# A two-layer hybrid decoder: norms by token halves, the last two FFN tiles projected down together

## The chip, the cores and the metric

The kernel runs on one core of a Trainium2 chip. The metric is the device time of one execution in microseconds. Before the change it is 2683.03 us, the median of 3 runs (2682.59 to 2683.53). The engines are PE (TensorE, matmuls), DVE (VectorE), ACT (ScalarE), POOL (GpSimd) and SP (SyncE, which here only issues transfers). Each has its own instruction queue, works it off in order, and waits for the others at semaphores.

## What is computed

Two layers over 1024 tokens with 1024 features, float32:

```python
for layer in range(DEPTH):                                   # DEPTH = 2
    hn = rms_norm(h, norm_mix_g[layer])
    h = h + hybrid_mixer(hn, ...)                            # @ w_in (3072 columns), attention and conv, @ w_out
    hn = rms_norm(h, norm_ffn_g[layer])
    h = h + conv_glu_ffn(hn, w_up[layer], conv_ffn_w[layer], w_down[layer])
return rms_norm(h, final_g)

def rms_norm(x, g, eps=1e-6):
    return x * rsqrt(mean(x * x, axis=-1) + eps) * g
def conv_glu_ffn(h, w_up, conv_w, w_down):                   # D_FF = 2816, 22 tiles of 128
    g, u = split(h @ w_up, 2)
    return (silu(causal_dwconv(g, conv_w)) * u) @ w_down
```

So there are five norms: before each mixer, before each FFN, and one over the result.

## The kernel before

**Layout.** `h` holds the state with features on the 128 partitions: `h[:, m, :]` is feature tile m (of 8), with all 1024 tokens along it. A matmul takes a 128 x 128 weight block and 512 tokens, so each token half t has its own PSUM bank (there are 8 banks of 512 float32). Every float32 product is made of three passes: w_hi x_hi, w_hi x_lo, w_lo x_hi (`three_pass`, L425 to L427). POOL splits each weight tile, 128 x 1024, into w_hi and w_lo (`split`, L349 and L351); there are two slots, so a tile is split only when the tile two places before it has been used up, and SP loads the raw tile into `stage` once its slot is free (L284). ACT makes x_hi = round(h * g) (`head_tile`, L665) and DVE makes x_lo = h * g - x_hi (`absorb`, L870).

**A norm.** The factor rstd per token is applied after the projection, as DVE takes a bank out (`evacuate`, L856: bank * rstd_all). So projection can begin before rstd is known, but its result can't leave PSUM. The order of a norm (`start_normed` on PE, `start_norm` on DVE): ACT squares the 8 feature tiles into 8 scratch tiles (L668), POOL adds them in five steps (`start_sums`, `end_sums`, L358), DVE does the last two adds (L900, L902), PE sums over the partitions by 8 one-column matmuls (`sum_squares`, L466), DVE computes rsqrt by 12 tiny operations (`rsqrt`, L881 to L894) and spreads it along a diagonal (L906), PE multiplies that by ones (`spread`, L473), and ACT copies the outcome to `rstd_all` (L672). Meanwhile PE does, for the first two weight tiles, all w_hi x_hi and w_lo x_hi (64 matmuls, L488 and L490), then waits for the sum, does w_hi x_lo (32, L499), and the spread. A third and a fourth tile follow (`project`), and need the slots of the first two.

**Start of a layer.** DVE takes out q and k of unit 0, rotates both (`rotate`, L914 to L919), takes out v, splits q and k (`keep_k`, `keep_rests`, up to L937) and raises `cur_ready`, for which the first scores wait. Then attention follows, where PE mixes scores, transposes and projections in a fixed order. At the very start ACT issues the loads of x by 8 feature tiles (L822), does two sines and an exponential for rotary tables and lambda, and then squares and heads in turn.

**FFN.** For tile f, PE projects gate and up (2 x 48 matmuls), DVE takes out the gate, ACT applies the centre tap (L809) and DVE the other two (L1103), ACT the silu (L814), DVE multiplies by up (L1114), ACT rounds to `mix_hi` (L816), DVE makes `mix_lo` (L1118, `mix_ready`). PE then projects down (`down`): 8 feature tiles x 2 halves x 3 passes, and DVE adds each to `h` (`add_down`, L875). Down of tile f - 1 is issued behind the projections of tile f, and DVE's 8 adds stand ahead of the product of tile f. Down of the last tile, 21, has nothing in front of it. Its banks are `DOWN` (2 to 7, in pairs).

**The end.** After the last down come squares, sums, rsqrt, spread, rstd, 8 output operations (L1199) and 8 transfers (L331).

## Time and profile before

| | |
|---|---|
| median of 3 runs | 2683.03 us |
| the profiled execution: its time / its span | 2682.59 / 2680.8 us |
| PE busy | 2531.5 us, 94% |
| DVE, POOL, ACT busy | 60%, 30%, 23% |
| granted PE clock, mean | 0.978 |
| chain that ended last | PE 82%, DVE 12%, ACT 3%, issue 2% |

PE's busy time counts matmuls from issue to their modelled end; those in a row overlap, so the distance between two starts is the figure to read. The granted clock is a share of 2.4 GHz: 0.50 is 1.2 GHz. In the 40 slices of the page (67 us each), PE stands at 6 tenths in the first and 4 in the last, and at 8 or 9 elsewhere. The time outside the span is 1.8 us.

### The profile page before, as it was taken

To read this page: it belongs to the slowest core of one execution; us is meant where nothing else is said; L and a number is where in the kernel's file an instruction comes from. 1 tells how busy PE (TensorE), PEld (TensorE's weight loads), DVE (VectorE), ACT (ScalarE), POOL (GpSimd) and SP (SyncE) were. 2 spreads that over 40 slices of the span, in tenths; PEclk is the share of its full clock that TensorE was granted. 3 is DMA by queue.
4 is the path that set the end of the run, shared out by engine and by line. 5 is a ranking of instruction groups with operands and counts; after the bars stand their busy time and mean duration, and the time that the engine had idled before them with its cause. 6 is when DMAs were issued, how large, how long until landed. Compare 5 with 4: busy or idle time off the path is not lost.

```text
span 2680.8 us, 29574 instructions
## 1 busy us (share of the span) xinstructions
PE 2531.5 (94%) x12006; PEld 2105.2 (79%) x12006; DVE 1603.8 (60%) x1979; ACT 624.3 (23%) x1161; POOL 815.4 (30%) x437
## 2 busy tenths in 40 slices
PE   6999998899999999999889999979999999999994
PEld 4888887777888888888678888868788888888883
DVE  6545677535556665566674467763465555666555
ACT  3344444321010010000224334443210001001002
POOL 4221213142333333333432111222433333333332
PEclk9999999999999999999999999989999999999997
DMA  3000001211111111111210000121111111111111
GB/s 129 32 24 32 24 32 40 74 48 40 47 48 48 50 53 47 47 48 47 102 40 24 32 24 32 32 79 41 38 45 54 48 48 48 48 50 52 48 40 63
DMA packets 50583, 127.32 MB, mean 47 GB/s; under 512 B 4496, under 2 KB 22032, under 8 KB 50448
## 3 DMA queue, kind: packets, MB, share of 16 engines
q1 hardware_dynamic: 47856, 120.05, 13.6%
q10 hardware_dynamic: 2592, 5.38, 0.5%
q8 instruction: 96, 1.57, 0.2%
q14 instruction: 39, 0.32, 0.0%
HBM read 116.76 MB, written 8.39 MB: 47 GB/s over the span
## 4 chain that ended last, share of the span: by engine, by line
PE 82%; DVE 12%; ACT 3%; issue 2%; POOL 0%; DMA 0%; DVEq 0%; ACTq 0%; POOLq 0%
PE ps L425 24%; PE ps L427 24%; PE ps L426 24%; PE ps L539 3%; DVE x_lo L870 3%; PE ps L526 2%; DVE h L916 2%; PE ps L499 1%; PE ps L513 1%; ACT prob L750 1%; PE ps L514 1%; DVE h L914 1%; DVE prob L950 1%; PE ps L466 1%; DVE q_next L917 0%
## 5 line engine op out<-in xcount | busy, mean ns | idle before, releaser
L425 PE MATMUL ps<-x_hi,w_hi 128*128 128x512 f32 x2304 | 910.8, 395 | 17.3 <-POOLq L354 8.9
L427 PE MATMUL ps<-x_hi,w_lo 128*128 128x512 f32 x2304 | 901.0, 391 | 0.0
L426 PE MATMUL ps<-x_lo,w_hi 128*128 128x512 f32 x2304 | 900.4, 391 | 0.0
L349 POOL CAST w_hi<-stage 128x1024 fp32r<-128x1024 f32 (+1 forms) x198 | 206.5, 1043 | 1749.2 <-PE ps L427 1661.2
L351 POOL TENSOR_TENSOR w_lo<-stage,w_hi 128x1024 fp32r<-128x1024 f32 (+1 forms) x198 | 522.0, 2636 | 15.8
L425 PEld LDWEIGHTS ps<-x_hi,w_hi 128*128 128x128 f32 x2304 | 434.4, 189 | 110.3 <-POOLq L354 13.1
L427 PEld LDWEIGHTS ps<-x_hi,w_lo 128*128 128x128 f32 x2304 | 434.2, 188 | 91.8
L426 PEld LDWEIGHTS ps<-x_lo,w_hi 128*128 128x128 f32 x2304 | 434.9, 189 | 87.0
L875 DVE TENSOR_TENSOR h<-ps,h 128x1024 f32<-128x1024 f32 x352 | 431.0, 1224 | 78.7 <-PE ps L427 38.8
L425 PE MATMUL ps<-q_split,w_hi 128*128 128x512 f32 x704 | 277.0, 393 | 10.7 <-DVE q_split L1118 10.7
L427 PE MATMUL ps<-q_split,w_lo 128*128 128x512 f32 x704 | 275.8, 392 | 0.0
L426 PE MATMUL ps<-q_split,w_hi 128*128 128x512 f32 x704 | 275.8, 392 | 0.0
L816 ACT ACTIVATE q_split<-k_next 128x1024 fp32r<-128x1024 f32 x44 | 46.7, 1061 | 720.9 <-DVEq L1116 720.9
L856 DVE TENSOR_TENSOR q_next<-ps,rstd_all 128x512 f32<-128x512 f32 x112 | 77.0, 691 | 226.4 <-PE ps L427 202.9
L1103 DVE SCALAR_TENSOR_TENSOR k_next<-padded,vec,k_next 128x1024 f32<-128x1024 f32 x88 | 176.7, 2008 | 57.8 <-ACT k_next L809 56.2
L856 DVE TENSOR_TENSOR padded<-ps,rstd_all 128x512 f32<-128x512 f32 x88 | 60.0, 685 | 200.7 <-PE ps L427 183.2
L750 ACT ACTIVATE prob<-prob,neg_top 128x128 f32<-128x128 f32 (+3 forms) x192 | 147.1, 770 | 125.2 <-DVE neg_top L950 124.9
L539 PE MATMUL ps<-v_cur,padded 128*128 128x64 f32 (+1 forms) x1152 | 152.9, 276 | 14.1 <-ACT padded L709 11.4
L425 PEld LDWEIGHTS ps<-q_split,w_hi 128*128 128x128 f32 x704 | 133.3, 189 | 41.5 <-issue 11.5
L539 PEld LDWEIGHTS ps<-v_cur,padded 128*128 128x128 f32 x1152 | 144.1, 193 | 20.5 <-ACT padded L709 14.6
L427 PEld LDWEIGHTS ps<-q_split,w_lo 128*128 128x128 f32 x704 | 133.1, 189 | 27.9
L426 PEld LDWEIGHTS ps<-q_split,w_hi 128*128 128x128 f32 x704 | 133.3, 189 | 27.3
(136 smaller groups left out, 2264.6 us busy)
## 6 DMA issues: line engine op xcount, KB each, us to landing
stage<-stream SPq DMA_DIRECT2D x180, 512.0 KB, 3.2
stage<-stream SPq DMA_DIRECT2D x16, 448.0 KB, 4.6
h<-x_t ACTq DMA_DIRECT2D x8, 512.0 KB, 9.3
h<-x_t SPq DMA_DIRECT2D x8, 512.0 KB, 3.3
saved_h<-h SPq DMA_DIRECT2D x8, 512.0 KB, 2.8
h<-saved_h SPq DMA_DIRECT2D x8, 512.0 KB, 3.3
out_t<-h SPq DMA_DIRECT2D x8, 512.0 KB, 3.0
stage<-stream SPq DMA_DIRECT2D x16, 64.0 KB, 4.7
```

Source lines behind the costliest of these rows:

```text
L349: pool.tensor_copy(w_hi[:, s, wide], stage[:, s, wide]).then_inc(pool_seq, 1)
L351: pool.tensor_tensor(w_lo[:, s, wide], stage[:, s, wide], w_hi[:, s, wide].bitcast(f32), ALU.subtract)\
L425: pe.matmul(out, w_hi[:, s, w], hi, start=start, stop=False)
L426: pe.matmul(out, w_hi[:, s, w], lo, start=False, stop=False)
L427: return pe.matmul(out, w_lo[:, s, w], hi, start=False, stop=stop)
L526: ended = pe.transpose(ps[:, TURNED, b * P:(b + 1) * P], prob[:, g % 2, j, (b0 + b) * P:(b0 + b + 1) * P], eye[:, :])
L539: ended = pe.matmul(ps[:, HEAD, at:at + wide], turned_groups[count % 2][:, (b - b0) * P:(b - b0 + 1) * P], v_cur[:, b, dims], start=b == 0 ...
L750: act.activation(scores, scores, ACT.Exp, bias=neg_top[:, g % 2, j:j + 1], scale=-1.0, accum_out=total[:, g % 2, j:j + 1]).then_inc(exp_do ...
L856: dve.tensor_tensor(out[:, halves_of_t[t]], bank(b), rstd_all[:, halves_of_t[t]], ALU.mult)\
L870: dve.scalar_tensor_tensor(x_lo[:, m, :], h[:, m, :], g_of(m), x_hi[:, m, :].bitcast(f32), ALU.mult, ALU.subtract).then_inc(x_lo_ready, 1)
L875: dve.tensor_tensor(h[:, m, :], bank(DOWN + 2 * (m % pairs), 2), h[:, m, :], ALU.add)\
L1103: dve.scalar_tensor_tensor(k_next[:, :], padded[:, TAPS - 1 - back:TAPS - 1 - back + SEQ], tap, k_next[:, :], ALU.mult, ALU.add).then_inc( ...
```

## The change

- **Norms by token halves.** Heads, rests, squares, sums, rsqrt, spread and rstd are done for tokens 0 to 511 (t = 0) and 512 to 1023 (t = 1) apart. PE's new order in `start_normed`: heads of tiles 0 and 1 for half 0, their rests, heads and rests of tile 0 for half 1, heads of tile 1, sum of half 0, rests of tile 1, and then the third tile's projection into banks 6 and 7 (`THIRD`), with spread of half 0, sum of half 1 and spread of half 1 put between its k steps. A first weight tile is free for its successor when three halves are done. rsqrt of half 1 (`end_norm`) comes on DVE after half 0 of the first tiles has been taken out.
- **Who adds squares.** At a layer's start DVE adds all eight (`partial(..., 1)`, seven half adds, each waiting for the one before). Before the FFN and at the end, POOL adds the first six and DVE two (`SUMMED` = 6); before the FFN POOL does this ahead of the splits of the first two FFN tiles.
- **The last two FFN tiles together.** `last_down`: down of tiles 20 and 21 is accumulated in one bank per feature tile, all 8 banks, first half 0 of tile 20 and of 21, then half 1; DVE adds halves. `mix_hi` and `mix_lo` alternate between two buffers.
- **The start.** x is loaded by SP in eight transfers, each of two feature tiles and one half, the first between the first two weight tiles; ACT does heads and squares before its sines. The rotary angles are computed on DVE between the two halves of `absorb`; lambda is computed after unit 0's q and k are ready. POOL clears the unused halves of k_lo. Between the FFN and layer 1 ACT does heads ahead of squares, by halves (`prepare_next`).
- **The end.** In the last layer, half 1's rows use banks 0, 1, 4, 5 in a ring, each row ended before the next; half 0's sum, spread and outputs lie between them. Outputs read the spread from PSUM, and leave in 16 transfers.

```diff
-            plan.append((layer, "tile", projection_tile(unit, group), "halves", halves + (2 if n == 0 else 0)))
+            plan.append((layer, "tile", projection_tile(unit, group), "halves", halves + (1 if n == 0 else 0)))
...
+            if f == F_TILES - 1:
+                plan.append((layer, "tile", down_tile(f - 1), "layers", layer + 1))
+            elif f:
                 downs += KT
                 plan.append((layer, "tile", down_tile(f - 1), "downs", downs))
-        downs += KT
+        downs += 2 * KT
...
+        ROW_BANKS, RING = (2, 3, 0, 1, 4, 5, 6, 7), (0, 1, 4, 5)
+
+        NORM, THIRD = (SCORE, SCORE + 1), (TURNED, HEAD)
...
-                    sp.wait_ge(add_done, (layer * F_TILES - 1) * KT + m + 1)
+                    sp.wait_ge(add_done, half_added(layer - 1, m, 1))
...
+            def load_x(t, m):
+                rows = x_t[m * P:(m + 2) * P, halves_of_t[t]].rearrange("(k p) t -> p k t", p=P)
+                sp.dma_start(h[:, m:m + 2, halves_of_t[t]], rows).then_inc(x_in[t][m // 2], 16)
+
             n = 0
             for layer in range(DEPTH):
-                for _ in range(2):
-                    load(n)
-                    n += 1
+                load(n)
+                if layer == 0:
+                    load_x(0, 0)
+                load(n + 1)
+                n += 2
                 if layer:
                     save_h(layer)
+                else:
+                    for t in range(2):
+                        for m in range(0, KT, 2):
+                            if t or m:
+                                load_x(t, m)
...
+            def sum_squares(norm, halves, parts):
+
+                for m in range(0, SUMMED, 2):
+                    for t in halves:
+                        pool.wait_ge(squares_ready[t], KT * norm + m + 2)
+                    add_squares(parts, m, m + 1)
+                    if m:
+                        add_squares(parts, 0, m)
                 pool.sem_inc(pairs_ready, 1)
...
+                for n in range(len(PROJECTIONS) + 1):
                     split()
+                    if layer == 0 and n == 1:
+
+                        pool.memset(k_lo[high, 0, :].bitcast(f32), 0.0).then_inc(zeros_ready, 1)
+                        pool.memset(k_lo[low, 1, :].bitcast(f32), 0.0).then_inc(zeros_ready, 1)
+                        pool.wait_ge(zeros_ready, 2)
                 pool.wait_ge(half_done, layer * LAYER_HALVES + PROJECTED)
                 for m in SPLIT_BY_POOL:
                     split_mix(layer, m)
                 for _ in range(len(OUT_TILES) - 1):
                     split()
-                sums_and_splits()
-                for _ in range(3 * F_TILES - 2):
+                sum_squares(2 * layer + 1, range(2), slice(0, SEQ))
+                for _ in range(3 * F_TILES):
                     split()
-            start_sums()
-            end_sums()
+            for t in range(2):
+                sum_squares(2 * DEPTH, (t,), halves_of_t[t])
...
+            def last_down(layer):
+                f = F_TILES - TOGETHER
+                tiles = (next_tile(), next_tile())
+                ready(tiles[0])
+                pe.wait_ge(mix_ready, seen(mix_ready))
+
+                pe.wait_ge(add_done, half_added(layer, 0, 0) - 1)
+                for m, b in enumerate(ROW_BANKS):
+                    take_bank(b)
+                    down_part(f, tiles[0], m, 0, b, True)
+                ready(tiles[1])
+                pe.wait_ge(mix_ready, seen(mix_ready))
+                for m, b in enumerate(ROW_BANKS):
+                    down_part(f + 1, tiles[1], m, 0, b, False).then_inc(down_done, 1)
+                if layer < DEPTH - 1:
+                    for m, b in enumerate(ROW_BANKS):
+                        pe.wait_ge(add_done, half_added(layer, m, 0))
+                        ended = down_part(f, tiles[0], m, 1, b, True)
+                    ended.then_inc(first_of_two, 1)
+                    for m, b in enumerate(ROW_BANKS):
+                        down_part(f + 1, tiles[1], m, 1, b, False).then_inc(down_done, 1)
+                else:
+                    for m in range(KT):
+                        if m == 2:
+                            sum_squares(0)
+                        if m == 5:
+                            spread(0)
+                        b = RING[m % len(RING)]
+                        if m < len(RING):
+                            pe.wait_ge(add_done, half_added(layer, ROW_BANKS.index(b), 0))
+                        else:
+                            pe.wait_ge(add_done, half_added(layer, m - len(RING), 1))
+                        down_part(f, tiles[0], m, 1, b, True)
+                        down_part(f + 1, tiles[1], m, 1, b, False).then_inc(down_done, 1)
+                down_tiles[0] += 2 * KT
...
+                for i in range(2):
+                    heads_of_x(i, 0)
+                for i in range(2):
+                    rests_of_x(i, 0)
+                heads_of_x(0, 1)
+                rests_of_x(0, 1)
+                heads_of_x(1, 1)
+                sum_squares(0)
+                rests_of_x(1, 1)
+                n = next_tile()
+                project_half(n, 0, THIRD[0], {3: lambda: spread(0), 6: lambda: sum_squares(1)})
+                if n < len(PROJECTIONS):
+                    pe.wait_ge(lam_exped, 1)
+                project_half(n, 1, THIRD[1], {5: lambda: spread(1)})
...
+                project()
+                project()
+                last_down(layer)
+            sum_squares(1)
+            spread(1)
...
             def prepare_loaded():
-                for m in range(KT):
-                    act.wait_ge(x_in[m], 16)
-                    square_tile(m, m)
-                    if KT // 2 <= m < KT - 1:
-                        head_tile(m - KT // 2, gain[:, m - KT // 2:m - KT // 2 + 1])
-                for m in range(KT // 2 - 1, KT):
-                    head_tile(m, gain[:, m:m + 1])
+                for t in range(2):
+                    for m in range(KT):
+                        act.wait_ge(x_in[t][m // 2], 16)
+                        head_tile(m, t, gain[:, m:m + 1])
+                    for m in range(KT):
+                        square_tile(m, m, t)
 
             def prepare_ffn(layer):
                 done = layer * LAYER_HALVES + PROJECTED + OUT_EARLY
+                last = OUT_ORDER[-1]
                 for p, m in enumerate(OUT_ORDER[:-1]):
-                    act.wait_ge(evac_done, done + 2 * p + 2)
-                    square_tile(p, m)
-                act.wait_ge(half_done, done + 2 * KT)
-                for m in OUT_ORDER[:3]:
-                    head_tile(m, gain_of(layer, V_FFN_G, m))
-                act.wait_ge(evac_done, done + 2 * KT)
-                square_tile(KT - 1, OUT_ORDER[-1])
-                for m in OUT_ORDER[3:]:
-                    head_tile(m, gain_of(layer, V_FFN_G, m))
+                    for t in range(2):
+                        act.wait_ge(evac_done, done + 2 * p + t + 1)
+                        square_tile(p, m, t)
+                for t in range(2):
+                    act.wait_ge(half_done, done + 2 * KT - 1 + t)
+                    for m in OUT_ORDER[:-1]:
+                        head_tile(m, t, gain_of(layer, V_FFN_G, m))
+                    act.wait_ge(evac_done, done + 2 * KT - 1 + t)
+                    head_tile(last, t, gain_of(layer, V_FFN_G, last))
+                    square_tile(KT - 1, last, t)
 
...
+            def partial(norm, t, first):
+
+                part = halves_of_t[t]
+                if first == SUMMED:
+                    dve.wait_ge(pairs_ready, {1: 1, 3: 2, 4: 3 + t}[norm])
+                for m in range(first, KT):
+                    dve.wait_ge(squares_ready[t], KT * norm + m + 1)
+                    added = dve.tensor_tensor(squares[0][:, part], squares[0][:, part], squares[m][:, part], ALU.add)
+                    if m < KT - 1:
+                        added.then_inc(dve_seq, 1)
+                        dve.wait_ge(dve_seq, seen(dve_seq))
+                added.then_inc(partial_ready, 1)
+
+            def roots(t):
                 dve.wait_ge(sum_done, seen(sum_done))
-                y = rsqrt(ps[:, HEAD, 0:QB], D_MODEL, NORM_EPS)
-                blocks = [P, QB, P]
-                dve.tensor_tensor(diagonal.rearrange("p (b q) -> p b q", q=P),
+                n = QB // 2
+                room = (rs[:, 0, 0:n], rs[:, 1, 0:n], ps[:, NORM[t], P:P + n])
+                y = rsqrt(ps[:, NORM[t], 0:n], D_MODEL, NORM_EPS, room)
+                blocks = [P, QB // 2, P]
+                dve.tensor_tensor(diagonal[:, halves_of_t[t]].rearrange("p (b q) -> p b q", q=P),
                                   eye[:, :].unsqueeze(1).broadcast_to(blocks), y.unsqueeze(2).broadcast_to(blocks),
                                   ALU.mult).then_inc(diag_ready, 1)
+
+            def end_norm():
+                roots(1)
                 dve.wait_ge(rstd_ready, seen(rstd_ready))
...
+                for t in range(2):
+                    if t:
+                        end_norm()
+                    for out, first_bank in ((q_next[:, :], PROJ), (k_next[:, :], SPARE)):
                         evacuate(t, out, first_bank + t)
                 if layer:
                     dve.wait_ge(h_saved[5], 16 * layer)
                 else:
                     dve.wait_ge(tables_in, 16 * 4)
                 rotate(q_next)
-                evacuate(0, v_next[:, :], PROJ)
+                evacuate(0, v_next[:, :], THIRD[0])
                 rotate(k_next)
-                evacuate(1, v_next[:, :], PROJ + 1)
+                evacuate(1, v_next[:, :], THIRD[1])
                 keep_k(attended)
                 keep_rests(attended)
...
+                for m in LATE[:-1]:
                     for t in range(2):
                         add_out(layer, m, t, PROJ + t)
-
-            def hidden(layer, f):
                 for t in range(2):
-                    evacuate(t, padded[:, TAPS - 1:], PROJ + t)
+                    add_out(layer, LATE[-1], t, PROJ + t)
+                    absorb(t, OUT_ORDER, lambda m: gain_of(layer, V_FFN_G, m))
+                for t in range(2):
+                    partial(2 * layer + 1, t, SUMMED)
+                    if t == 0:
+                        roots(0)
+                dve.wait_ge(rstd_ready, seen(rstd_ready))
...
+            def hidden(layer, f):
+                gate, up = padded[:, TAPS - 1:], q_next[:, :]
+                if f:
+                    for t in range(2):
+                        evacuate(t, gate, THIRD[t] if f == 1 else PROJ + t)
+                    convolve_gates(layer, f)
+                    for t in range(2):
+                        evacuate(t, up, PROJ + t)
+                else:
+                    for t in range(2):
+                        if t:
+                            end_norm()
+                        evacuate(t, gate, PROJ + t)
+                        evacuate(t, up, SPARE + t)
+                    convolve_gates(layer, f)
+                if 0 < f < F_TILES - 1:
+                    for m in range(KT):
+                        add_down(m)
+                value()
+                value_rest(f)
+
+            def next_norm(layer):
+                dve.wait_ge(add_done, adds[0])
+                for t in range(2):
+                    for m, b in enumerate(ROW_BANKS):
+                        add_half(t, m, b)
+                    absorb(t, range(KT), lambda m: gain_of(layer, V_NEXT_G, m))
+                partial(2 * layer + 2, 0, 1)
+                roots(0)
+                partial(2 * layer + 2, 1, 1)
+                dve.wait_ge(rstd_ready, seen(rstd_ready))
+
+            def last_norm():
+                def out(t, rows):
+                    for m in rows:
+                        dve.scalar_tensor_tensor(h[:, m, halves_of_t[t]], h[:, m, halves_of_t[t]],
+                                                 gain_of(DEPTH - 1, V_NEXT_G, m), bank(NORM[t]),
+                                                 ALU.mult, ALU.mult).then_inc(out_ready, 1)
+
+                def add_ends(rows):
+                    for m in rows:
+                        add_half(1, m, RING[m % len(RING)])
+
+                dve.wait_ge(add_done, adds[0])
+                for m, b in enumerate(ROW_BANKS):
+                    add_half(0, m, b)
+                partial(2 * DEPTH, 0, SUMMED)
+                add_ends((0, 1))
+                roots(0)
+                add_ends((2, 3, 4, 5))
+                dve.wait_ge(spread_done, seen(spread_done, 2 * 2 * DEPTH + 1))
+                out(0, (0, 1))
+                add_ends((6,))
+                out(0, (2, 3))
+                add_ends((7,))
+                out(0, (4, 5, 6, 7))
+                partial(2 * DEPTH, 1, SUMMED)
+                roots(1)
+                dve.wait_ge(spread_done, seen(spread_done))
+                out(1, range(KT))
```

## Rows read from the trace of the kernel before

**Rows 1.** PE's waits, whole run: for whom: us, times, longest.
```profile
PE ps L466 <- DVE q_next L902: 22.0, 5, 11.5
PE ps L488 <- ACT x_hi L665: 21.5, 9, 15.1
```

**Rows 2.** Timeline, PE after the first norm: start us, duration us, engine, line, operation.
```profile
59.02 0.63 PE L425 MATMUL ps<-x_hi,w_hi 128*128 128x512 f32 x1
59.45 0.63 PE L426 MATMUL ps<-x_lo,w_hi 128*128 128x512 f32 x1
...
70.07 0.39 PE L425 MATMUL ps<-x_hi,w_hi 128*128 128x512 f32 x1
70.30 0.39 PE L426 MATMUL ps<-x_lo,w_hi 128*128 128x512 f32 x1
```

**Rows 3.** Timeline of the start, all engines (square brackets: idle before, and releaser).
```profile
6.42 2.34 POOL L351 TENSOR_TENSOR w_lo<-stage,w_hi 128x1024 fp32r<-128x1024 f32 x1
...
14.16 1.05 ACT L668 ACTIVATE q_next<-h 128x1024 f32<-128x1024 f32 x1
...
20.18 0.77 PE L488 MATMUL ps<-x_hi,w_hi 128*128 128x512 f32 x1 [15.08 <-ACT x_hi L665]
...
59.83 1.35 DVE L914 STREAM_SHUFFLE h<-q_next 128x1024 f32<-128x1024 f32 x1
```

**Rows 4.** The page's part 6: DMA issues, KB each, median us to landing.
```profile
h<-x_t ACTq DMA_DIRECT2D x8, 512.0 KB, 9.3
```

**Rows 5.** Groups by line and shape: busy us, mean ns, idle before.
```profile
L1103 DVE SCALAR_TENSOR_TENSOR k_next<-padded,vec,k_next 128x1024 f32<-128x1024 f32 x88 | 176.7, 2008 | 57.8 <-ACT k_next L809 56.2
...
L358 POOL TENSOR_TENSOR q_next<-q_next,k_next 128x1024 f32<-128x1024 f32 x5 | 11.9, 2389 | 35.9 <-ACT k_next L668 35.4 <-POOL w_lo L351 0.5
```

**Rows 6.** One line, L870: duration in ns, least, median, most; first and last start.
```profile
L870 DVE SCALAR_TENSOR_TENSOR x_lo<-h,vec,x_hi x24: 1271/1284/3433, 591.9 to 1919.4; 128x1024 fp32r<-128x1024 f32 x24
```

**Rows 7.** Timeline, first seam from the output projection to the FFN, all engines.
```profile
579.89 1.04 POOL L349 CAST w_hi<-stage 128x1024 fp32r<-128x1024 f32 x1 [7.36 <-PE ps L427]
...
590.74 0.69 DVE L863 TENSOR_TENSOR h<-ps,h 128x512 f32<-128x512 f32 x1 [4.75 <-PE ps L427]
...
610.40 2.36 PE L466 MATMUL ps<-ones,q_next 128*128 128x1 f32 x16 [1.85 <-DVE q_next L902]
...
612.63 10.35 PE L499 MATMUL ps<-x_lo,w_hi 128*128 128x512 f32 x32
...
624.73 1.02 ACT L672 ACTIVATE rstd_all<-ps 128x1024 f32<-128x1024 f32 x1 [24.68 <-PE ps L473]
...
636.77 1.22 DVE L1118 TENSOR_TENSOR q_split<-k_next,q_split 128x1024 fp32r<-128x1024 f32 x1 [1.18 <-ACT q_split L816]
...
637.91 1.28 DVE L856 TENSOR_TENSOR padded<-ps,rstd_all 128x512 f32<-128x512 f32 x2
...
640.47 3.47 DVE L1103 SCALAR_TENSOR_TENSOR k_next<-padded,vec,k_next 128x1024 f32<-128x1024 f32 x2 [1.28 <-ACT k_next L809]
...
651.30 10.74 DVE L875 TENSOR_TENSOR h<-ps,h 128x1024 f32<-128x1024 f32 x8 [0.67 <-PE ps L427]
```

**Rows 8.** Timeline, seam from layer 0's FFN to layer 1, PE and DVE.
```profile
1319.36 0.76 PE L425 MATMUL ps<-q_split,w_hi 128*128 128x512 f32 x1 [5.78 <-DVE q_split L1118]
...
1373.37 1.38 DVE L914 STREAM_SHUFFLE h<-q_next 128x1024 f32<-128x1024 f32 x1 [0.36 <-issue]
```

**Rows 9.** Window there: us; PE, PEld, DVE, ACT, POOL busy; clock, DMA, GB/s.
```profile
1319.40:1325.00 5.60, 5.60 (x13) 4.40 (x14) 1.37 (x2) 1.06 (x1) 0.00 (x0) 0.50 0.12 46
```

**Rows 10.** Timeline of the end, PE and DVE.
```profile
2629.60 0.76 PE L425 MATMUL ps<-q_split,w_hi 128*128 128x512 f32 x1 [4.90 <-DVE q_split L1118]
...
2654.32 3.57 PE L466 MATMUL ps<-ones,q_next 128*128 128x1 f32 x16 [11.51 <-DVE q_next L902]
...
2661.61 3.78 PE L473 MATMUL ps<-prob,ones 128*128 128x512 f32 x4 [3.72 <-DVE prob L906]
...
2666.49 9.65 DVE L1199 SCALAR_TENSOR_TENSOR h<-h,vec,rstd_all 128x1024 f32<-128x1024 f32 x8 [4.93 <-ACT rstd_all L672]
```

339 lines of the change are left out of this document (166 added, 173 removed).

## The prediction

> **What bounds the kernel now.** I read the waits of TensorE (PE) first [rows 1]. PE is busy for 94% of the span, and outside attention its idle time lies almost wholly at five seams: the start, twice from the output projection to the FFN, once from layer 0's FFN to layer 1, and the end. So the matmuls themselves, 0.227 us apart when back to back at full clock [rows 2], stay; what can be won is idle time at seams and what follows it: after an idle spell the same matmuls are 0.427 us apart [rows 2]. In one such spell, behind a wait of 5.78 us, 13 matmuls took 5.60 us at a granted clock of 0.50, the lower level, 1.2 GHz [rows 8, 9]; at full pace 13 take 2.95. So I price the slow spell behind a long wait at 2.6 us.
>
> Then the timelines of the seams. In each, PE runs 64 matmuls on x_hi, waits for the sums of squares, runs 16 one-column matmuls, 32 matmuls on x_lo, the spread, and waits for a split by POOL. In the first mix-to-FFN seam the sum waits 1.85 us and takes 2.36, and the 32 take 10.35 instead of 7.25, since the clock has dropped [rows 7]. The Vector engine (DVE) waits all that time for rstd. At the end everything behind the last projection is serial.
>
> **The change, part by part.** I follow each seam: PE's matmuls at 0.227, DVE at 0.69 us for a 512-wide operation and 1.22 for a 1024-wide one [rows 7], POOL at 2.39 for a 1024-wide add [rows 5]. ACT takes 1.02 for a 1024-wide copy from PSUM [rows 7]; for 512 I take 0.6 (half, and a tenth). A sum of squares over one half is 4 one-column matmuls, a quarter of 2.36 to 3.57 [rows 7, 10], so 0.75; a spread of one half is half of 3.78 cold [rows 10] and, by pitch, 0.95 warm. One rsqrt with its diagonal takes 3.6 us at the end (the 16 end at 2657.9, the spread starts at 2661.6 [rows 10]); with half the diagonal 3.0.
>
> *The start.* PE waits 15.08 us for the first x_hi, since ACT first takes its sines and all squares begin at 14.16 [rows 3]. The first weight tile is split at 8.8 [rows 3]. After: x_hi comes first and by halves. PE starts near 8.4, when the first tile is split, at the slow pitch; it is held by tile 1's split (3.4 later) and by the arriving x. The eight transfers of x took a median of 9.3 us from their issue [rows 4], all being in flight together; half the bytes of x are now wanted first, and I take the last of them at 12 (an estimate), 15 as the worse bound, which would cost 2.5. So both heads of half 0 end at 18.2. Rests of half 0: 16 matmuls, 21.8. ACT does 8 squares before the heads of half 1, which end at 22.1; PE ends heads and rests of tile 0 at 27.4, heads of tile 1 at 31.0, sum 31.8. DVE's rsqrt ends at 35.2; its seven chained half adds of squares for half 1 (0.69 + 0.03 each, 5.0) come only behind it, 40.2, where PE, which comes at 38.6, waits 1.7. Sum 41.1, two k and five k of tile 2 (21 matmuls) 45.8, spread 46.8, rstd 47.4, two evacuations 48.7. There the rotation of q starts; before it starts at 59.83 [rows 3]: 11.1. From there DVE's work to the first masked scores is the same, plus six tiny lambda operations (0.2 each), less about 0.6 that DVE waited for PE. So 10.5 us are won at the first scores. But PE is through with its two further tiles at 58, some 10 us before DVE has split q and k: the wait for sums turns into a wait for `cur_ready`, and a slow spell follows, 2.5. Net 8.0.
>
> *Mix to FFN, twice.* POOL's five sums come ahead of the splits of the FFN's first tiles. POOL is idle there for 7.36 us up to 579.9 [rows 7], so they start at 572.5; they take 12 (5 of 2.39) and the first split ends near 588, before PE needs it at 590.7 (DVE's last add starts at 590.74 [rows 7]); were it late by x, PE would wait x. The last output tile's half 0 gets its x_hi while half 1 is projected. PE: 48 matmuls to 602, 40 more to 611.0, sum 611.8, rests 613.6, and then, with sums and spreads in gaps that now hold matmuls of tile 2, spread of half 1 at 625.3, rstd 625.9. Before, rstd is there at 625.75 [rows 7]: no gain on DVE, but PE has tile 2 done at 627.3 instead of 637.7 (its evacuation starts at 637.91 [rows 7]). Now DVE decides. Gate and up of half 1 (1.3), the centre tap (1.3), two taps 4.0 [rows 5], silu, product, rounding, rest (four operations of 1.06 to 1.22, with their handovers 5.1) give the first hidden tile at 637.7, against 638.0 before (636.77 + 1.22 [rows 7]). Only then are the gates of tile 1 taken out of the third pair of banks, for which the first down projection waits: 639.1, where PE is ready at 638.2. DVE then needs tap 1.2, taps 3.47 [rows 7], two evacuations and one add, so its first add ends at 646.4, while PE after three of eight rows (4.1 us, 643.2) needs that bank: a wait of 3.2 and a slow spell, of which I take 1.2 for a short wait. Rows end at 654.4, the adds at 655.8; before at 662.04 (651.30 + 10.74 [rows 7]). 6.2 us each, 12.4. Bounds: without POOL in DVE's way (two taps in 2.6) the wait is 1.7 and the gain 9.8; with both pairs of taps at 5.0 and a full slow spell, 2.3.
>
> What two 1024-wide taps cost depends on POOL: the same x_lo operation takes 1.271 us at best and 3.433 at worst [rows 6]. The Trainium skill, SBUF — State Buffer, section Who interferes with whom, says that a DVE operation with two SBUF inputs is blocked for a whole POOL instruction that reads SBUF. By that rule a pair of taps could take 2.6 + 2.4 = 5.0 us instead of the 4.0 and 3.47 that I take from the rows, and the two seams would give 5 us less; the slowest single operation in the rows fits it (1.27 + 2.16). The change also cuts 1024-wide operations in two. The skill's VectorE: DVE Perf Modes, section The TRN2 errata, names 151 cycles for each instruction, 0.16 us, which on some 20 split operations on paths would be 3 us; the rows show 1.28 for two of 512 in a row against 1.22 for one of 1024 [rows 7].
>
> *FFN to layer 1.* Before, PE waits 5.78 us for the last hidden tile, up to 1319.36, and runs slow for 5.6 us [rows 8, 9]; down(20), 48 matmuls, lies before the wait, so the last projection ends at 1302.7. After: tile 20, half 0 (24 matmuls) needs only hidden 20, which is old, ends at 1308.3; hidden 21 is ready near 1308, as DVE no longer has 8 adds (10.7) in front of it. No wait. Four times 24 matmuls end at 1324.8. Heads and rests as above: the 88 to 1344.9, sum 1345.7, rsqrt 1349.2, half 1's seven adds 1354.2 (PE waits 1.7), spread 1360.8, rstd 1361.4, rotation from 1362.7 instead of 1373.37 [rows 8]. 10.6 won, and again some 10 us of PE waiting for `cur_ready` and the slow spell: 8.1. The saves of h move ahead of the next weight load in SP's queue; they start with half 1's adds and should be through by 1340, where the load for tile 2 is needed at 1341. If not, that wait is up to 3 us. The clear of k_lo, now on POOL, I cost at nothing: POOL waits for PE there.
>
> *The end.* Before, the last projection ends at 2613.8 (2629.60 less 4.90 and 48 matmuls [rows 10]), the span at 2680.8. The wait of 4.90 goes, and its slow spell. Then half 0: two tiles 2625.0; its squares by ACT behind the adds, POOL's five half adds to 2628.2, partial 2629.7, sum 2630.5 between rows 1 and 2 of half 1; spread at 2635.5, all rows of half 1 at 2639.6. DVE, in its order, ends half 0's eight outputs at 2644.3, partial of half 1 2645.8, sum 2646.8, rsqrt 2649.8, spread (cold, 1.9) 2651.7, eight outputs at 0.68 2657.2, and the last transfer as before: the last output ends at 2676.14 (2666.49 + 9.65 [rows 10]) and the span at 2680.8, 4.7. End 2661.9: 18.9 won. Bounds: 15 if half 0's outputs push half 1's sum back, 21 if none of DVE's work stands in its way.
>
> **Sum.** 8.0 + 12.4 + 8.1 + 18.9 = 47.4 us. The profiled execution took 2682.59 (span 2680.8), so 2635.2; against the median of 2683.03, 2635.6. I say 2636.
>
> **Rivals.** (a) *PE's pace decides, not DVE's chain*: the two waits for `cur_ready` cost no slow spell and POOL stays out of DVE's way: 10.5 + 19.6 + 10.6 + 21 = 61.7, 2621. For it: in attention's first steps PE also waits for others. Against: each long idle spell in the trace is followed by the slow pitch. (b) *The half norms gain nothing before rstd*: in-order DVE and ACT take back in each layer start what the halves give, as I find for the FFN seam's rstd itself. Left are the end (15 to 19), the wait and slow spell at the FFN's end (8.4), and 4 for the start's earlier x: 28 to 31, 2653. (c) *Slower*: at both layer starts PE idles 10 us and then feeds on small matmuls of attention; if the clock stayed at 1.2 GHz for all of unit 0, its 8 half tiles (192 matmuls) would cost 0.2 more each, 38 us a layer, 77 in all, 2713. It decides from 26 us a layer (47.4 and 5.4 over two), 132 matmuls at the slow pitch. Against it: the spell of [rows 9] was over after 5.60 us. The skill's TensorE: Matmul & The Clock Gate, section HAM oscillation, describes a kernel whose clock fell again at every gap; in this trace one spell follows one gap. (d) *It does not do what it says*: a wait in the new order binds each half to the other, as in (b) with the end's gain halved: 20, 2663.
>
> **How the numbers follow.** Forecast 0.58 (2627 to 2646), (a) 0.15, (b) 0.18, (c) 0.03, (d) 0.06. To hold 8 in 10 the range takes in (a) and (b): 2616 to 2656. A measurement of this kernel tells about 0.2%, 5.4 us, from no change. Faster 0.96, same 0.01, slower 0.03.
>
> **What would show it.** In the changed trace: the first projection matmul near 8.4; no wait for the last hidden tile; a new wait of some 10 us ahead of the first scores of both layers, with a granted clock of half behind it; a wait of 2 to 3 us within the first down projection of each FFN, for DVE's add; the wait for the sum at the end gone, half 0's outputs under half 1's work. Wrong it would be if rstd of half 1 came later than I say (DVE's order), if saves held the weight load, or if POOL's sums delayed the split at the FFN seams.

## The result, and the profile after

| | before | changed |
|---|---|---|
| median | 2682.81 us | 2656.99 us (4 runs, 2655.39 to 2659.75) |
| ratio, 95% interval | | 0.9905 (0.9893 to 0.9918) |
| profiled execution: time / span | 2682.59 / 2680.8 us | 2659.75 / 2657.9 us |
| granted PE clock, mean | 0.978 | 0.978 |

The change wins 26 us, not the 47 forecast, and ends just above the range. The page of the changed kernel:

```profile
PE 2526.0 (95%) x12006; PEld 2106.5 (79%) x12006; DVE 1615.5 (61%) x2113; ACT 631.0 (24%) x1229; POOL 790.5 (30%) x434
...
PE 82%; DVE 12%; ACT 2%; issue 2%; POOL 1%; DMA 0%; DVEq 0%; POOLq 0%
```

Nothing here says where the time went; PE's waits do (for whom: us in total, times, longest). The 15.1 us for x_hi and the 11.5 for the sum of [rows 1] are gone, two waits of 11.4 for the splits of q and k are new (DVEq: DVE's sequencer, which raises `cur_ready`), and the longest wait for a sum is 5.8:

```profile
PE ps L598 <- DVEq L1055: 22.8, 2, 11.4
PE ps L537 <- DVE q_next L1006: 15.4, 5, 5.8
...
PE ps L451 <- DVE h L969: 6.6, 2, 3.3
```

To place the miss I cut each span at eight instants of DVE's timeline: the first masked scores of a layer, the add of the last output tile's half 0, the last add of the first down projection, the end of the last up evacuation. "Forecast" is the before column with the prediction's terms taken off. Each column is one profiled execution; that of the changed kernel was the slowest of its four, 2.8 us above their median.

| stretch, us | before | forecast | changed |
|---|---|---|---|
| start to first masked scores | 82.4 | 71.9 | 82.7 |
| attention, layer 0 | 502.9 | 505.4 | 505.4 |
| output projection to first down, layer 0 | 76.8 | 70.6 | 72.3 |
| rest of the FFN | 641.4 | 641.4 | 641.4 |
| to layer 1's first masked scores | 91.3 | 80.7 | 87.1 |
| attention, layer 1 | 503.3 | 505.8 | 505.1 |
| output projection to first down, layer 1 | 75.1 | 68.9 | 72.4 |
| rest of the FFN | 641.4 | 641.4 | 641.4 |
| end | 66.3 | 47.4 | 50.3 |

Of the 24.5 us missed in this execution (21.4 by the medians), 10.7 lie in the start, 6.3 at layer 1's start, 1.7 and 3.5 at the FFN seams, 2.9 at the end, and attention gives 0.7 back. Two of these are questions for experiments: why do the layer starts give 4 us instead of 21, and is it the same cause elsewhere?

The start in the changed kernel, DVE and POOL (start us, duration us; L1006 is the half add of squares, L377 and L379 POOL's split, L1031 the sine product of the rotation):

```profile
29.16 4.92 DVE L1006 TENSOR_TENSOR q_next<-q_next,prob 128x512 f32<-128x512 f32 x3
...
38.20 0.68 DVE L1006 TENSOR_TENSOR q_next<-q_next,k_next 128x512 f32<-128x512 f32 x1
38.91 1.41 DVE L1006 TENSOR_TENSOR q_next<-q_next,v_next 128x512 f32<-128x512 f32 x1
40.36 2.75 DVE L1006 TENSOR_TENSOR q_next<-q_next,v_cur 128x512 f32<-128x512 f32 x1
43.15 0.69 DVE L1006 TENSOR_TENSOR q_next<-q_next,padded 128x512 f32<-128x512 f32 x1
43.87 2.15 DVE L1006 TENSOR_TENSOR q_next<-q_next,prob 128x512 f32<-128x512 f32 x3
...
59.60 3.30 DVE L1031 TENSOR_TENSOR h<-h,sin_t 128x1024 f32<-128x1024 f32 x1
```
```profile
29.33 1.42 POOL L377 CAST w_hi<-stage 128x1024 fp32r<-128x1024 f32 x1 [14.52 <-PE ps L571]
30.83 2.70 POOL L379 TENSOR_TENSOR w_lo<-stage,w_hi 128x1024 fp32r<-128x1024 f32 x1
38.22 1.56 POOL L377 CAST w_hi<-stage 128x1024 fp32r<-128x1024 f32 x1 [4.68 <-PE ps L571]
39.86 2.71 POOL L379 TENSOR_TENSOR w_lo<-stage,w_hi 128x1024 fp32r<-128x1024 f32 x1
58.30 1.04 POOL L377 CAST w_hi<-stage 128x1024 fp32r<-128x1024 f32 x1 [15.74 <-PE ps L453]
59.42 2.40 POOL L379 TENSOR_TENSOR w_lo<-stage,w_hi 128x1024 fp32r<-128x1024 f32 x1
```

Beside each of these splits by POOL one or two of DVE's operations are long: 2.75 us for an add that takes 0.69 alone. Between the two norm halves PE frees a weight slot, and that lets POOL start just as DVE sums half 1.

At layer 1 there is a second thing. DVE has summed half 0 by 1336.8 and stands idle for 8 us until PE comes to that sum, though ACT has all squares of half 1 ready at 1329; only then come rsqrt and half 1's adds:

```profile
1334.66 2.15 DVE L1006 TENSOR_TENSOR q_next<-q_next,prob 128x512 f32<-128x512 f32 x3
...
1347.22 0.69 DVE L1018 TENSOR_TENSOR prob<-eye,ps 128x512 f32<-128x512 f32 x1
...
1348.55 2.74 DVE L1006 TENSOR_TENSOR q_next<-q_next,v_next 128x512 f32<-128x512 f32 x1
...
1365.51 1.32 DVE L1029 STREAM_SHUFFLE h<-q_next 128x1024 f32<-128x1024 f32 x1
```

### The profile page after: what moved, and what is told of

Its sections match the earlier page's. It is cut to its first block, busy times and chain, and to the rows that moved or that the text cites. A ratio compares the mean times of both kernels' runs of the same rounds, so it can differ in the third digit from the quotient of the medians.

```text
span 2657.9 us, 29833 instructions
## 1 busy us (share of the span) xinstructions
PE 2526.0 (95%) x12006; PEld 2106.5 (79%) x12006; DVE 1615.5 (61%) x2113; ACT 631.0 (24%) x1229; POOL 790.5 (30%) x434
## 4 chain that ended last, share of the span: by engine, by line
PE 82%; DVE 12%; ACT 2%; issue 2%; POOL 1%; DMA 0%; DVEq 0%; POOLq 0%
PE ps L451 24%; PE ps L453 23%; PE ps L452 23%; PE ps L624 3%; PE ps L611 2%; DVE h L1031 2%; PE ps L598 1%; PE ps L599 1%; ACT prob L843 1%; DVE h L1029 1%; DVE q_next L1006 1%; PE ps L571 1%; DVE prob L1065 1%; PE ps L561 1%; DVE k_next L1229 1%
## 5 line engine op out<-in xcount | busy, mean ns | idle before, releaser
L377 POOL CAST w_hi<-stage 128x1024 fp32r<-128x1024 f32 (+1 forms) x198 | 207.6, 1048 | 1787.7 <-PE ps L453 1711.7
L379 POOL TENSOR_TENSOR w_lo<-stage,w_hi 128x1024 fp32r<-128x1024 f32 (+1 forms) x198 | 524.5, 2649 | 15.9
L969 DVE TENSOR_TENSOR h<-ps,h 128x1024 f32<-128x1024 f32 x320 | 391.4, 1225 | 64.7 <-PE ps L453 28.3
L802 ACT ACTIVATE padded<-ps 128x512 f32<-128x512 f32 (+2 forms) x192 | 94.4, 492 | 256.1 <-PE ps L611 255.6
L451 PE MATMUL ps<-q_split,w_hi 128*128 128x512 f32 x352 | 139.9, 398 | 8.6 <-DVE h L969 6.6
L452 PE MATMUL ps<-q_split,w_hi 128*128 128x512 f32 x352 | 138.6, 394 | 0.0
L453 PE MATMUL ps<-q_split,w_lo 128*128 128x512 f32 x352 | 138.6, 394 | 0.0
L451 PE MATMUL ps<-k_twice,w_hi 128*128 128x512 f32 x352 | 137.6, 391 | 0.6 <-DVE k_twice L1243 0.6
L452 PE MATMUL ps<-k_twice,w_hi 128*128 128x512 f32 x352 | 137.2, 390 | 0.0
L453 PE MATMUL ps<-k_twice,w_lo 128*128 128x512 f32 x352 | 137.2, 390 | 0.0
```

Source lines behind the costliest of these rows:

```text
L377: pool.tensor_copy(w_hi[:, s, wide], stage[:, s, wide]).then_inc(pool_seq, 1)
L379: pool.tensor_tensor(w_lo[:, s, wide], stage[:, s, wide], w_hi[:, s, wide].bitcast(f32), ALU.subtract)\
L451: pe.matmul(out, w_hi[:, s, w], hi, start=start, stop=False)
L452: pe.matmul(out, w_hi[:, s, w], lo, start=False, stop=False)
L453: return pe.matmul(out, w_lo[:, s, w], hi, start=False, stop=stop)
L802: act.activation(turned_groups[turned[0] % 2][:, 0:size], ps[:, TURNED, 0:size], ACT.Copy)\
```

## The experiments

What follows is compared with the changed kernel's 2657 us. The runs bear on five things: DVE's order, POOL's splits at the layer starts, the slow spell behind PE's new wait, the order of the end, and the FFN seam.

**The kernel as it is, as the yardstick.**

> The changed kernel again, unedited, as the yardstick for the runs beside it: 2655 to 2660 us, first masked scores of layer 0 at 82.7 us and of layer 1 at 1388.8 us by its trace (cumulative gain over the kernel before: -0.2 and 5.95 us).

2656.93 us, 0.9911 (0.9896 to 0.9926). Its stretches are those of the table, except that the first masked scores come at 80.1 instead of 82.7: among the eight profiled executions that share the start's order they came between 80.0 and 82.7, so a single span settles nothing below 3 us; stretches between two instants do. The difference doesn't come in with x: PE is through with half 0's x_hi at 20.1 us here and at 19.9 in the table's execution. It arises behind that: DVE's seven adds took 7.0 us here and 7.7 there, and from half 1's sum to the rotation it was 10.5 here and 12.1 there, where PE ran at the slow pitch for longer.

**DVE sums half 1 ahead of half 0's rsqrt, layer 1 only.**

```
 partial(2 * layer + 2, 0, 1)
-roots(0)
 partial(2 * layer + 2, 1, 1)
+roots(0)
```

> Only at the seam from layer 0's FFN to layer 1, DVE adds the squares of half 1 right behind those of half 0, ahead of rsqrt of half 0, in the 8.05 us for which it is idle there. Theory L (half 1's adds are late because of their place behind rsqrt of half 0, and PE's slow spell follows the wait): PE's wait of 3.21 us for the sum of half 1 goes, the slow spell behind it (2.1 us) too, DVE's adds no longer meet POOL's fourth split (2 us), so the rotation of q starts near 1361 us instead of 1365.5, and the kernel takes 4 to 5 us less. Rival R (PE's pace and DVE's chain behind rstd decide): PE's wait goes, but the first masked scores of layer 1 stay within 1 us of 1388.8, and the time within 1 us.

2653.59 us, 0.9896 (0.9881 to 0.9911), 3.3 less. The adds run in DVE's former idle time, PE no longer waits for that sum, and from the last up evacuation to the rotation it is 58.7 us instead of 63.8; the prediction had 59.3. The stretch to the first masked scores falls from 87.1 to 82.0.

**POOL holds two splits at each layer start.**

```
 for n in range(len(PROJECTIONS) + 1):
+    if n == 3: pool.wait_ge(partial_ready, 4 * layer + 2)
+    if n == 4: pool.wait_ge(cur_ready, layer * ATTENDING + 1)
     split()
```

> At both layer starts POOL holds the split of the fourth projection tile back until DVE has added the squares of half 1, and the fifth and later ones until the first q and k are split. Theory P (POOL's splits hold DVE's operations with two SBUF inputs): the seven adds of half 1 take 5.0 us instead of 7.7 (start) and 7.0 (layer 1), the sine product of q 1.2 instead of 3.3, and the casts and last add of k 3 us less in all; first masked scores 8 us earlier at the start and 7 us at layer 1, of which up to 2 us each is given back where PE then waits for the fifth tile's split; 8 to 14 us in all. Rival R (the length of DVE's operations does not decide, PE's order does): the operations are shorter, the time is within 2 us.

2645.40 us, 0.9866 (0.9851 to 0.9880), 11.5 less: the largest share by far. In its trace the seven adds take 5.05 us, as the prediction had costed them, and PE's wait for the sum is 1.16:

```profile
38.46 0.69 DVE L1010 TENSOR_TENSOR q_next<-q_next,v_next 128x512 f32<-128x512 f32 x1
39.19 0.69 DVE L1010 TENSOR_TENSOR q_next<-q_next,v_cur 128x512 f32<-128x512 f32 x1
39.92 0.69 DVE L1010 TENSOR_TENSOR q_next<-q_next,padded 128x512 f32<-128x512 f32 x1
40.64 2.15 DVE L1010 TENSOR_TENSOR q_next<-q_next,prob 128x512 f32<-128x512 f32 x3
...
53.09 1.22 DVE L1035 TENSOR_TENSOR h<-h,sin_t 128x1024 f32<-128x1024 f32 x1
```
```profile
42.85 1.04 POOL L377 CAST w_hi<-stage 128x1024 fp32r<-128x1024 f32 x1 [9.77 <-DVE q_next L1010]
```

The sine product is 1.22 instead of 3.30, and PE's wait for the splits 7.0 instead of 11.4. The released splits then hit the next thing on DVE, the six lambda operations on one column, which the prediction had at 0.2 each:

```profile
69.42 1.02 DVE L1341 TENSOR_TENSOR vec<-heads 128x1 f32<-128x1 f32 x1
70.48 0.16 DVE L1344 TENSOR_TENSOR vec<-vec 128x1 f32<-128x1 f32 x1
70.67 2.19 DVE L1347 TENSOR_TENSOR vec<-vec 128x1 f32<-128x1 f32 x1
```
```profile
69.39 1.04 POOL L377 CAST w_hi<-stage 128x1024 fp32r<-128x1024 f32 x1 [23.03 <-DVEq L1059]
70.51 2.34 POOL L379 TENSOR_TENSOR w_lo<-stage,w_hi 128x1024 fp32r<-128x1024 f32 x1
```

An operation on 128 values is held about as long (1.02 and 2.19 us) as one on 65,536 (2.75): what is paid is POOL's instruction, not the size of DVE's.

**POOL adds six of the squares at the layer starts, as at the other norms.**

```
+if n == 1:
+    for t in range(2):
+        sum_squares(2 * layer, (t,), halves_of_t[t])
```

(in POOL's loop of splits; DVE's partials then start from the seventh square.)

> At both layer starts POOL adds the first six squares of each half (five half adds of 1.3 us), as it does at the other norms, in its idle time behind the second split, and DVE only the last two. Theory L: DVE's adds of half 1 shrink from 7.7 and 7.0 us to 1.4 (up to 3.5 if they meet a split), PE waits for neither sum, so no slow spell; first masked scores earlier by 6 to 9 us at the start and 4 to 6 us at layer 1, 10 to 15 us in all. Rival (POOL becomes the late one): its sums of half 1 end after the slot of the third tile is free, the third tile's split and with it PE's third projection come 1 to 3 us later, and the gain is under 5 us.

2650.91 us, 0.9889 (0.9872 to 0.9905), 6.0 less, from layer 1 (82.6 instead of 87.1) and from places where nothing was edited (1.5 us at the first FFN seam, 1.4 at the end; see the clock, below). At the start it costs: the sums hold DVE's making of x_lo, so PE waits five times for it, and the first masked scores come at 83.1. DVE's two adds there take 3.46 us beside POOL's split. So POOL's sums hold DVE as its splits do.

**All three at the layer starts**: the order, the held splits, and the lambda operations moved into DVE's wait for half 1's rstd.

```
 def end_norm(lam=False):
     roots(1)
+    if lam: lambdas()
```

> Edit: three in one at the layer starts: half 1's squares are summed on DVE ahead of the rsqrt of half 0 at layer 1; POOL holds its split of the fourth projection tile until half 1's squares are summed and the next until q and k are split; the six lambda operations of layer 0 move into DVE's wait for the rstd of half 1. Theory (POOL's splits beside DVE's chain, and DVE's order, are what the two layer starts lost): holding alone gave 11.5 us and the order alone 3.3. With the order, DVE no longer waits for the sum of half 0, 3 us at layer 1 on top of holding; with the lambdas moved, 2 to 4 at layer 0, up to where PE's wait there ends. 5 to 7 below the kernel with holding alone: 2639. Rival (PE's own weights, split late, take over): 2645, with waits of PE for weights in unit 0.

2635.46 us, 0.9825 (0.9810 to 0.9839), 21.5 less than the changed kernel. The first masked scores come at 72.1 and layer 1's 77.6 after the last up evacuation (forecast: 71.9 and 80.7). The six lambda operations take 0.15 or 0.16 each where they now stand. Their move was not run alone; at the start, where the order edit changes nothing, the first masked scores come 3.4 us before those of the kernel that only holds POOL.

**The price of the slow spell: PE fed during its wait for q and k.**

```
+take_bank(SPARE + 1)
+for _ in range(20):
+    pe.matmul(bank(SPARE + 1), ones[:, :], diagonal[:, halves_of_t[1]], start=True, stop=True)
```

> Edit: at both layer starts PE, before it waits for the splits of q and k, runs 20 matmuls on ones and the diagonal into a bank that nobody reads (their results are unused; fp32, so they take longer than the fp32r ones). The price of the slow spell behind the wait for the splits is read from this. If each spell costs what the prediction says, 2.5 us, and the fill keeps the clock up to the first scores: 5 us less, 2652. If the spell behind the wait lies beside a chain that DVE sets (scores that wait for reductions), it costs nothing at the end of the layer, and the time stays at 2657 within 1; if the fill ends too early the spell stays and the window behind the wait shows 0.50 again, with the same time.

2659.68 us, 0.9914 (0.9899 to 0.9928), 2.7 more. The fill took 17.33 us and outlasted the wait, so the scores began 5.2 us late at both layers; attention then took 502.3 and 502.7 us instead of 505.2 and 505.0. The median says little here: the four times are 2655.3, 2656.8, 2662.6 and 2662.9, and the trace is of one of the long ones. The attention stretches give a slow spell a price of 2 to 3. With 12 matmuls:

> Edit: as the fill of 20 matmuls, with 12, which should end about when q and k are split (20 took 17.3 us and outlasted the wait; 12 take 10.4 of 11.4). If the slow spell behind the wait costs 2.5 us each, both waits together give 5, less up to 1 where the fill outlasts the wait at one start: 2652 against 2656.7. If the spell is hidden beside DVE's chain: within 1 of 2656.7. The long fill lost 5 us at each start to its own length and the total rose by 3 only, which speaks for a price of some 3 to 4 us each.

2656.19 us, 0.9903 (0.9889 to 0.9918), no difference that can be told. At layer 0 the fill ended 1.1 us before the scores, PE then waited 1.9 for DVE's first reduction, and the clock fell after that wait instead. At layer 1 the two waits were 1.07 and 0.79, and the clock stayed up (the last row):

```profile
78.00:80.00 2.00, 0.63 (x4) 0.52 (x4) 1.79 (x8) 0.00 (x0) 0.00 (x0) 1.00 0.00 0
80.00:84.00 4.00, 3.37 (x15) 3.33 (x16) 1.63 (x10) 1.35 (x6) 0.00 (x0) 0.57 0.00 0
...
1386.00:1388.00 2.00, 2.00 (x15) 1.95 (x16) 1.05 (x7) 1.37 (x6) 0.00 (x0) 1.00 0.00 0
```

(windows; the third figure from the end is the granted clock.) So this run moved the spell at layer 0 and removed it at layer 1, where attention took 503.6 instead of 505.0. In the kernel with all edits of the starts and the end, with 7 matmuls of fill:

> Edit: the kernel with all edits of the starts and the end, and 7 matmuls of fill ahead of PE's wait for q and k (7.1 us there). If a slow spell costs 2.5 us also where the wait is shorter: 2626 against 2631. If the spell costs nothing because DVE's chain paces the first steps of attention: 2631.

2629.92 us, 0.9804 (0.9789 to 0.9818), against 2630.84 without the fill: 0.9 less, not told apart. At layer 0 the clock did stay up. These are the 7 us from the first score on, without the fill and then with it; behind each, that first score and the first transposition of a later step, which has the same work in front of it in both:

```profile
71.71:78.71 7.00, 6.70 (x24) 5.94 (x25) 2.54 (x12) 3.21 (x11) 6.52 (x4) 0.50 0.22 77
...
71.71 0.45 PE L602 MATMUL ps<-k_twice,q_split 128*128 128x128 f32 x1 [7.11 <-DVEq L1061]
...
82.77 0.27 PE L615 MATMUL ps<-eye,prob 128*128 128x128 f32 x1
```
```profile
70.14:77.14 7.00, 5.97 (x33) 4.98 (x34) 2.54 (x12) 3.22 (x11) 6.52 (x4) 1.00 0.24 75
...
70.14 0.30 PE L602 MATMUL ps<-k_twice,q_split 128*128 128x128 f32 x1 [1.03 <-DVEq L1064]
...
79.12 0.27 PE L615 MATMUL ps<-eye,prob 128*128 128x128 f32 x1
```

It takes 11.06 us to get there without the fill and 8.98 with it. Matmul by matmul, that lead of 2.1 us is still there after the 1500th, 275 us on, so no later wait takes it back; it shrinks to 1.3 between 380 and 410 us, where PE waits long in both runs and the clock is low behind it in both. Layer 0's attention ends 1.1 us sooner. At layer 1, behind waits of 0.91 and 0.79, the clock fell after all (0.76 over the same 7 us), the lead is 0.4 to 0.7, and attention gains 0.3. In the run with 12 matmuls, layer 1's lead over the yardstick is 2.4 after the 22nd matmul and 1.4 at the end. A slow spell here costs PE 2.1 to 2.5 us, then. In these two places 1.1 and 1.4 of it are left at the end of attention; with the fill of 20, at layer 1, it was 2.3.

**The end: half 0's last four outputs behind half 1's sum.**

```
-out(0, (4, 5, 6, 7))
 partial(2 * DEPTH, 1, SUMMED)
+out(0, (4, 5))
 roots(1)
+out(0, (6, 7))
```

> Edit: at the end, DVE sums half 1's squares before the last four of half 0's outputs; two of these go into the wait for the sum and two into the wait for the spread. Theory (half 0's outputs push half 1's sum back, the bound of 15 us that the prediction named against 18.9): DVE's two adds come 2.7 us earlier less what ACT's last squares and POOL's last sum still take, about 0.6: 1.5 to 2.2 us less, 2655. Rival (POOL's last sum or ACT's last square sets it): within 0.5 of the changed kernel, 2657.

2655.72 us, 0.9900 (0.9885 to 0.9915), 1.2 less, within the noise of the total. The stretch of the end falls from 50.3 to 47.8, and PE's wait for half 1's sum from 5.83 to 3.33. Since an unedited end was seen at 47.3 as well (below), the wait is the better witness: 2.5 us.

**The same, and half 0's sum ahead of row 4 instead of row 2, its spread ahead of row 6.**

> Edit: the end as in the kernel that sums half 1's squares before the last four outputs of half 0, and besides PE takes half 0's sum of squares ahead of row 4 of half 1 in place of row 2, and the spread ahead of row 6 in place of row 5. Theory (the wait of 2.7 us for POOL's and DVE's sums, and the ten slow matmuls behind it, hold the rows of half 1, and with them half 1's sum): the wait is covered by rows 2 and 3, no slow pitch follows, rows end about 4.5 us earlier, and 3 to 4 of it reach half 1's sum: from the last up projection to the end 45 us, where the changed kernel takes 51 and the one with the outputs behind takes 48.5; total about 2652. Rival (half 0's rsqrt and outputs, not the rows, keep DVE busy up to half 1's sum): rows end earlier but the sum doesn't, 2655 or more.

2651.39 us, 0.9884 (0.9868 to 0.9901), 5.5 less than the changed kernel; the end takes 43.7 us. In the changed kernel PE waits 2.68 us for half 0's sum and is slow behind it; here that wait is gone:

```profile
2623.81 1.86 PE L537 MATMUL ps<-ones,q_next 128*128 128x1 f32 x8 [2.68 <-DVE q_next L1006]
2642.82 1.87 PE L537 MATMUL ps<-ones,q_next 128*128 128x1 f32 x8 [5.83 <-DVE q_next L1006]
```
```profile
2626.62 1.12 PE L543 MATMUL ps<-prob,ones 128*128 128x512 f32 x2 [0.28 <-DVE prob L1018]
2635.14 1.56 PE L537 MATMUL ps<-ones,q_next 128*128 128x1 f32 x8 [4.64 <-DVE q_next L1006]
```

(changed kernel above, this one below.) The end's order, then, was worth 6.6 us more than the change took from it; against the shortest end that was seen without these edits, 47.3, it is 3.7.

**Both sets of edits.**

> Edit: the three edits of the layer starts and the two of the end in one kernel. They lie in different stages, so they should add: 2635.5 less what the end's two give (4.5 us): 2631. If the end's gain were only an earlier start of the same wait, 2635.

2630.84 us, 0.9809 (0.9795 to 0.9824). 21.5 and 5.5 were won apart, 26.1 together: they add.

**The FFN seam: the early gate, and POOL held.** The prediction's first down projection should begin 1.0 us after PE is ready for it, since the gates of tile 1 come out late.

```
 convolve_gates(layer, 0)
+for t in range(2):
+    evacuate(t, gate, THIRD[t])
```

(and no longer ahead of tile 1's own taps.)

> Edit: in each FFN, DVE takes the gates of tile 1 out of the third pair of banks right behind the taps of tile 0, while ACT does its silu, and not behind the first hidden tile; the taps of tile 1 themselves stay where they are. Theory (the first down projection is held by the order on DVE): the wait of 1.04 us before it goes; the gates' 1.28 us fall into DVE's idle 1.18 behind its taps, so the first add comes 1.1 to 1.3 earlier and the 3.3 us wait at row four shrinks to 2.2. 1 to 1.5 us for each FFN: 2 to 3 us less than the changed kernel, 2654. Rival (what is late is DVE's taps, and the silu's handover waits): the hidden tile comes later by what the gates take, and nothing is won, 2657.

2656.58 us, 0.9903 (0.9887 to 0.9920): nothing. The wait of 1.04 fell to 0.25 and the one at row four rose from 3.31 to 4.07, because the second pair of taps met POOL's next split and took 4.65 us instead of 3.84. So POOL was held for the first down tile:

```
+if n == 4: pool.wait_ge(conv_ready, layer * F_TILES + 1)
 split()
```

> Edit: in each FFN POOL holds its split of the first down tile until the taps of the first hidden tile are done. Theory (POOL's split beside the taps is what the mix-to-FFN seam lost): the pair takes 2.6 us instead of 4.62, the first hidden tile comes 2.0 earlier, the held split ends 3.5 behind the taps, about when ACT's silu, DVE's product, ACT's rounding and DVE's rest end, so PE isn't held by it; some 1.5 to 2 us for each FFN from the last output tile to the last add of the first down projection (72.1 to about 70.3), 3 to 4 in all, 2653. Rival (the held split collides with the product and the rest instead, or PE waits for it): the pair is 2.6 but the product or the rest grows by as much, 2656 to 2657.

2655.89 us, 0.9901 (0.9884 to 0.9919): nothing either. The first pair of taps is short, and the rest (2.15 instead of 1.23) and the second pair pay:

```profile
631.63 2.60 DVE L1231 SCALAR_TENSOR_TENSOR k_next<-padded,vec,k_next 128x1024 f32<-128x1024 f32 x2 [1.28 <-ACT k_next L904]
...
637.83 2.15 DVE L1245 TENSOR_TENSOR q_split<-k_next,q_split 128x1024 fp32r<-128x1024 f32 x1 [1.19 <-ACT q_split L911]
...
642.46 4.62 DVE L1231 SCALAR_TENSOR_TENSOR k_next<-padded,vec,k_next 128x1024 f32<-128x1024 f32 x2 [1.28 <-ACT k_next L904]
```
```profile
641.48 1.04 POOL L377 CAST w_hi<-stage 128x1024 fp32r<-128x1024 f32 x1 [2.58 <-PE ps L455]
642.60 3.40 POOL L379 TENSOR_TENSOR w_lo<-stage,w_hi 128x1024 fp32r<-128x1024 f32 x1
```

The rival stood: the collision moved. Holding a second split as well (the third gate tile, until the second taps are done), in the kernel with all other edits, and then with the early gate too:

> Edit: the kernel with the edits of the layer starts and the end, and POOL held in each FFN for the first down tile until the taps of tile 0 are done and for the third gate tile until those of tile 1 are. The second pair of taps takes 3.84 beside POOL there; held it should take 2.6 too, so the first add of the down projection comes 1.2 earlier again and the wait of 3.3 us at its row four shrinks. Theory: 3 us for each FFN, 2625 against 2631. Rival (the third gate tile, split after the taps, holds PE behind the down projection): 2628 or more, with a wait of PE for POOL there.

> Edit: that kernel and the early gate of tile 1. Alone the early gate gained nothing (the first down projection began only 0.1 us earlier within its seam, since the taps of tile 1 came no earlier). Theory (DVE's taps set the first add, not the gate's place): the same as with the holds alone, 2625 within 1. Rival (once the taps are short the gates' 1.3 us decide): 2623.

2626.70 us, 0.9793 (0.9778 to 0.9809), and 2626.37, 0.9793 (0.9778 to 0.9809): 4.1 and 4.5 below the kernel without holds. Both pairs of taps now take 2.60. Without holds that kernel's seams took 70.7 and 70.8 us, with the clock up; here they take 70.1 and 70.0, and 68.7 and 68.6 with the early gate. The last step is again the clock: it fell behind waits of 2.07 and 2.04 us in the one run and not behind waits of 2.04 and 1.92 in the other, so the gate's own worth is not shown. Where the clock stayed up in both, the seams differ by 2.1 us each, 4.2 in all, which fits the totals. The version with the early gate is the fastest, 30.6 us below the changed kernel and 56 below the one before.

**The clock behind a short wait.** Three stretches that share their code differ by 1.4 us from one execution to the next: 70.7, 72.1 or 73.5 at the FFN seam, 47.3, 48.9 or 50.3 at the end. The kernel with the held layer starts shows two of these in one execution. Both layers have the same wait of 3.29 us for the same add; then the window of each, layer 0 first:

```profile
642.32 0.50 PE L455 MATMUL ps<-q_split,w_hi 128*128 128x512 f32 x1 [3.29 <-DVE h L973]
...
1938.49 0.79 PE L455 MATMUL ps<-q_split,w_hi 128*128 128x512 f32 x1 [3.29 <-DVE h L973]
```
```profile
642.30:644.30 2.00, 1.98 (x9) 1.63 (x10) 2.00 (x2) 0.00 (x0) 0.00 (x0) 1.00 0.00 0
...
1938.50:1940.50 2.00, 2.00 (x5) 1.61 (x6) 2.00 (x2) 0.00 (x0) 0.00 (x0) 0.50 0.00 0
```

At 1.00 (2.4 GHz) PE starts nine matmuls in 2 us, at 0.50 (1.2 GHz) five; the seams are 70.75 and 73.52 us long. In the yardstick it was in between, 72.1.

## Why the prediction missed, step by step

*The start (forecast −10.5 at the first masked scores, measured +0.2, and −2.3 in the yardstick).* What failed is the step "its seven chained half adds of squares for half 1 (0.69 + 0.03 each, 5.0)" and, before it, the sum of half 0 at 31.0. DVE's work was costed with POOL absent, and no slow pitch of PE behind these waits. The sum of half 0 came 3.1 late (34.1). Of that, 1.7 was there before: PE began at 9.3 and not 8.4, half 0's last x came at 14.3 and not 12 (near the bound of 15 that the prediction named), and its heads ended at 19.9 instead of 18.2. The rest is a wait of 1.35 for DVE, whose last three adds took 4.92 us. Half 1's adds took 7.7 instead of 5.0, so its sum began 5.8 late (46.1). From there to the rotation it was 12.1 instead of 8.4, as PE ran at the slow pitch behind its waits of 1.35 and 2.35 us: the sum took 1.7 and the 21 matmuls 7.3, where the prediction had 0.75 and 4.7. The rotation came 9.5 late (58.2), and 1.3 more was lost from there on. The prediction had the price in its hand: two taps at 4.0 instead of 2.6 [rows 5] and x_lo at up to 3.43 [rows 6] were POOL's doing, and it used them at the FFN seams alone. What it left out is the trigger. In [rows 3] POOL's splits lay beside other work; the new order frees a slot of weights between the two halves of the norm, and the split starts just there.

The Trainium skill, SBUF — State Buffer, section Who interferes with whom, says that a DVE operation with two SBUF inputs is blocked for a whole POOL instruction that reads SBUF. The trace agrees: an add that takes 0.69 alone took 2.75 when it began 0.5 us into a POOL instruction of 2.71, and it ended 0.5 after it. The prediction took it as a rival for taps; it belonged to every such operation on the path.

With the three edits the first masked scores came at 72.1, the forecast's 71.9, but by two differences that cancel: the rotation began at 53.1 and not at 48.7, and from there DVE took 18.9 us instead of the 23.2 that the prediction carried over, since the 22.6 of the kernel before, from which it came, had POOL beside it too (two casts took 3.7 us there and 1.4 here), and the lambda operations, 1.2 of it, had moved.

*FFN to layer 1 (forecast −10.6, measured −4.3).* The half that removed the wait for the last hidden tile held: PE waits 0.31 us there instead of the 5.78 of [rows 8]. What failed is again "half 1's seven adds 1354.2 (PE waits 1.7)", and not their place: behind a sum for which DVE idled 8 us they began within 0.3 of the forecast, set off from the last up evacuation, but they took 7.0 instead of 5.0. PE waited 3.2 instead of 1.7, and its slow pitch, which the prediction had left out, cost 2.2 up to the rotation. The rotation to the first masked scores took 23.3 instead of before's 21.4, with POOL beside the sine product (3.35). These four add up to the miss. The place was not a miss but a chance: with the order alone the rotation comes 0.6 us before the forecast, and the prediction wrote the order down without asking what DVE did before it. The saves of h held nothing: between 1327 and the sum PE has no wait.

*The new wait for `cur_ready`.* Forecast some 10 us, measured 11.4 twice, with a clock of 0.50 behind it at both layers. Its price of 2.5 us fits the stretch (+2.6 and +1.8), and where a fill kept the clock up PE gained 2.1 to 2.5 in the first matmuls of attention. This term held, and its cause with it. Of that gain 1.1 to 2.3 were left at attention's end; what decides the loss at the long waits there is open.

*Mix to FFN (forecast −6.2 each, measured −4.5 and −2.7).* The wait at row four was forecast at 3.2 and measured 3.29, and no split was late by more than 0.85. Layer 0's seam took 72.3 against a forecast of 70.6. The taps were 4.62 and 3.86 instead of 4.0 and 3.47, 1.0 us more. Yet with the same taps the unedited seam took 70.7 in other runs, where the clock stayed up, so by how much the taps and by how much the slow spell (put at 1.2 for a short wait) was mis-sized can't be told apart: the spell alone moves the seam between 70.7 and 73.5. The further 1.8 at layer 1 is a size read off one row and used twice: before, that seam was 75.1 there and not 76.8 [rows 7].

*The end (forecast −18.9, measured −16.0).* The mechanism held: no long wait behind the last projection, half 0's outputs under half 1's work. The mis-sized term is the middle. The prediction's own times leave PE idle ahead of half 0's sum, from 2627.7 (two rows behind 2625.0) to 2629.7, and it gave this wait neither a name nor a slow spell. PE waited 2.68 us; behind that the sum took 1.7 instead of 0.75 and ten matmuls ran at the slow pitch, 2.0 more. Set off from the last up evacuation, half 1's rows ended 4.3 later than forecast, its sum began 3.9 later, and the end came 2.9 later. The wait for half 1's sum itself, 5.83 us, is what the prediction's times give (6.2). Its bound ("15 if half 0's outputs push half 1's sum back") names the right step; 16 was won.

*Chances.* The measured time lies 1 us above the range, whose upper end stood on rival (b), 2653 with 0.18, which came closest. That closeness is partly luck: (b) gave nothing to the FFN seams, where 7.2 us were won, and its cause, DVE's order, was worth 3.3 us, where POOL's splits, which it does not name, were worth 11.5.

## What to carry to other kernels

When a chain on DVE is moved or cut in two, draw POOL's instructions beside it as the new order releases them, and charge each collision with up to the whole POOL instruction; a small DVE operation pays as much as a large one. Holding POOL's splits until the chain is through gave 11.5 us here, but it must clear the whole chain: where only one was held, the next operations paid. And when two halves share one in-order engine, place the second half's ready work ahead of the first half's wait.

## What the runs showed of the hardware that was not expected

- DVE operations on 128x1 take 0.15 to 0.16 us alone, and 1.02 and 2.19 beside POOL's cast and its 2.34 us subtraction.
- The harm can be mutual: POOL's subtraction of a 128x1024 tile takes 2.34 to 2.42 us alone and 3.39 to 3.46 beside two taps of DVE.
- After the same wait of 3.29 us in one execution PE's clock stood at 1.00 once and at 0.50 once, and single seams differ by 1.4 us steps for it. Changes below some 3 us can't be read from one span.
- A fill of matmuls that ends a microsecond early keeps the clock or not by what follows: behind waits of 1.1 and 1.9 us it fell to half, behind 1.07 and 0.79 and behind 1.03 and 0.75 it stayed at 1.00, and behind 0.91 and 0.79 it fell later on (0.76 over 7 us).
- Two microseconds won by PE's clock in the first steps of attention were still there 275 us on.
